# Chunk loop of a hybrid block: state-space output written channel by channel, two heads in the two column halves of TensorE, row factors loaded, no transposes of y

## The reference, cut to what matters

```python
lmat = jnp.exp(jnp.where(causal, seg, -jnp.inf))
scores = jnp.einsum('bclgn,bcsgn->bcgls', cc, bc)
y_diag = jnp.einsum('bcgrls,bcsgrp->bclgrp', scores[:, :, :, None] * lmat, xc)
...
y_off = jnp.einsum('bclgn,bcgrpn,bcgrl->bclgrp', cc, prev, jnp.exp(a_cum))
return (y_diag + y_off).reshape(bsz, s, h, pd)
...
y = y + d_skip.astype(f32)[:, None] * xh
y = y.reshape(bsz, s, SSM_D_INNER) * jax.nn.silu(z.astype(f32))
```

## Time and profile before

| | |
|---|---|
| median of 3 runs | 2541.73 us (2538.14 to 2541.93) |
| profiled execution, span from first to last instruction | 2534.6 us |
| its own time beyond the span | no row gives it; the runs' median stands 7.1 us above the span |
| TensorE busy | 2436.9 us, 96% of the span |
| VectorE, GpSimd, ScalarE busy | 1538.6, 1266.1, 822.5 us |
| mean granted TensorE clock | 0.989 of full |

### The profile page before, as it was taken

The page is one execution under the profiler, slowest core; times in us unless marked ns, Lnnn a source line. Parts: engine busy times, 40 slices in busy tenths (PEclk is TensorE's granted clock), DMA queues, the critical chain, the costliest instruction groups (busy, mean ns, idle before and its releaser), DMA issues. The chain is left out here.

```text
span 2534.6 us, 29658 instructions
## 1 busy us (share of the span) xinstructions
PE 2436.9 (96%) x11540; PEld 2011.4 (79%) x11540; DVE 1538.6 (61%) x1411; ACT 822.5 (32%) x965; POOL 1266.1 (50%) x687
## 2 busy tenths in 40 slices
PE   7999999899999999989999899999999999999998
PEld 6888887677778888878878678888888878888776
DVE  4977997325766567653244897677677652323575
ACT  5234443445412232331013543333333321000332
POOL 2337887544445455443353266556556543333563
PEclk9999999999999999999999999999999999999999
DMA  6222334698676667745232222222222243122332
GB/s 230 92 84 92 108 120 135 216 267 283 202 209 168 187 173 215 178 141 174 100 133 83 100 83 75 74 98 75 74 97 76 100 174 116 50 83 84 131 101 108
DMA packets 293607, 335.34 MB, mean 132 GB/s; under 512 B 44461, under 2 KB 249594, under 8 KB 289402
## 3 DMA queue, kind: packets, MB, share of 16 engines
q1 hardware_dynamic: 260650, 271.42, 34.4%
q10 hardware_dynamic: 32848, 62.40, 6.7%
HBM read 230.50 MB, written 103.28 MB: 132 GB/s over the span
## 5 line engine op out<-in xcount | busy, mean ns | idle before, releaser
L498 PE MATMUL ps<-act_hi,w_hi 128*128 128x512 f32 x1328 | 532.4, 401 | 13.3 <-ACT ring_b L1212 4.8
L483 POOL TENSOR_SCALAR w_hi<-w_raw 128x1024 fp32r<-128x1024 f32 x123 | 145.0, 1179 | 764.0 <-issue 688.4
L502 PE MATMUL ps<-act_hi,w_lo 128*128 128x512 f32 x1328 | 518.4, 390 | 0.0
L501 PE MATMUL ps<-act_lo,w_hi 128*128 128x512 f32 x1328 | 517.9, 390 | 0.0
L485 POOL TENSOR_TENSOR w_lo<-w_raw,w_hi 128x1024 fp32r<-128x1024 f32 x123 | 328.6, 2672 | 10.3
L498 PEld LDWEIGHTS ps<-act_hi,w_hi 128*128 128x128 f32 x1328 | 250.0, 188 | 71.6 <-issue 8.1
L502 PEld LDWEIGHTS ps<-act_hi,w_lo 128*128 128x128 f32 x1328 | 249.8, 188 | 53.1
L501 PEld LDWEIGHTS ps<-act_lo,w_hi 128*128 128x128 f32 x1328 | 250.1, 188 | 52.3 <-issue 3.3
L2036 POOL TENSOR_TENSOR w_lo<-sm,w_hi 128x512 fp32r<-128x512 f32 x120 | 209.1, 1743 | 113.9 <-ACT w_hi L2390 113.9
L2036 POOL TENSOR_TENSOR w_lo<-w_raw,w_hi 128x512 fp32r<-128x512 f32 x90 | 139.3, 1549 | 151.8 <-ACT w_hi L2390 151.8
L2152 PE MATMUL ps<-t,w_hi 128*128 128x512 f32 x480 | 186.9, 389 | 0.2 <-POOL w_lo L2036 0.2
(11 more groups left out here) (393 smaller groups left out, 5130.9 us busy)
## 6 DMA issues: line engine op xcount, KB each, us to landing
w_raw<-in_w_in_dram SPq DMA_DIRECT2D x34, 1024.0 KB, 6.0
spill<-ring_a ACTq DMA_DIRECT2D x36, 512.0 KB, 2.6
w_raw<-in_w_ffn_down_dram SPq DMA_DIRECT2D x18, 1024.0 KB, 5.0
w_raw<-in_w_ffn_up_dram SPq DMA_DIRECT2D x16, 1024.0 KB, 5.2
w_raw<-in_w_ffn_gate_dram SPq DMA_DIRECT2D x16, 1024.0 KB, 5.2
f_cm<-ring SPq DMA_DIRECT2D x32, 512.0 KB, 2.6
spill<-ring_b ACTq DMA_DIRECT2D x31, 512.0 KB, 6.9
qkv_a<-spill SPq DMA_DIRECT2D x7, 1536.0 KB, 8.4
```

The lines of the kernel that those rows point to most:

```text
L483: nc.gpsimd.tensor_scalar(hi, raw, 1.0, 0.0, ALU.mult, ALU.add).then_inc(split_done, 1)
L498: first = nc.tensor.matmul(o, wh, mov[0][:, k, c], start=(k == 0), stop=False)
L501: nc.tensor.matmul(o, wh, mov[1][:, k, c], start=False, stop=False)
L502: last = nc.tensor.matmul(o, wl, mov[0][:, k, c], start=False, stop=(k == KD - 1))
```

## The change

- `diag` now has `xc[:, h]` (64 columns) as stationary and `dec[:, h]` as moving operand; head h writes output partitions 0 to 63 or 64 to 127 by its parity. All 16 heads stand in one piece. `off` gives channels on partitions too, as 8 products instead of 2.
- The factor `exp(a_cum)` is no longer per partition. So ScalarE writes it once, ahead of the loop, to a scratch tensor `exp_rows`, and SP loads 8 rows of it to each half of `zt`, repeated over 64 partitions (`load_e`). `zt` is used twice a chunk: first for this factor, then for z, whose load moves up in the queue.
- VectorE adds `diag` in one instruction; the 8 transposes and their semaphore go.

```diff
@@ PE
-        def diag(c, g):
-            for i in range(HPG):
-                h = g * HPG + i
-                last = t.matmul(bank(PB, 2)[:, i * P:(i + 1) * P], dec[:, h, :],
-                                xc[:, h - h % 2:h - h % 2 + 2, :].rearrange("p h d -> p (h d)"), start=True, stop=True)
+        def diag(c):
+            for h in range(SSM_HEADS):
+                d = slice(SSM_HEAD_DIM * (h % 2), SSM_HEAD_DIM * (h % 2) + SSM_HEAD_DIM)
+                last = t.matmul(bank(PB, 2)[d, h // 2 * P:(h // 2 + 1) * P], xc[:, h, :], dec[:, h, :], start=True, stop=True)
             last.then_inc(diag_done, 1)
...
-            for g in range(SSM_GROUPS):
-                last = t.matmul(bank(PC + g), xbc[:, KD + 2 + g, :], of_group(s_ssm, g), start=True, stop=True)
+            for k in range(KD):
+                last = t.matmul(bank(PC, 2)[:, k * P:(k + 1) * P], s_ssm[:, 2 * k:2 * k + 2, :].rearrange("p h d -> p (h d)"),
+                                xbc[:, KD + 2 + k // 4, :], start=True, stop=True)
...
-            diag(c, 0)
+            diag(c)
             gemm(steps[1])
-            after(pe, y_sum, c * 3 + 2)
-            diag(c, 1)
+            after(pe, y_sum, c * 2 + 1)
...
-            after(pe, o_sum, c * 2 + 2)
-            for k in range(KD):
-                last = t.transpose(bank(PA, 2)[:, k * P:(k + 1) * P], ysum[:, k * P:(k + 1) * P], ident[:, :])
-            last.then_inc(yt_done, 1)
...
-                after(pe, y_mid, c * 2 + 1)
+                after(pe, o_sum, c * 2 + 2)
                 scores(c + 1)
@@ SP
         def load_dec(c):
-            after(sp, diag_done, c * 2)
+            after(sp, diag_done, c)
...
+        def load_e(c):
+            after(sp, y_mid, c * 2)
+            for i in range(2):
+                rows = exp_rows[ROW_DT + i:ROW_DT + SSM_HEADS:2, tokens(c)]
+                sp.dma_start(zt[64 * i:64 * i + 64, :, :], rows.unsqueeze(0).broadcast_to([64, KD, P])).then_inc(in_e, 16)
+
         def load_z(c):
-            after(sp, y_mid, c * 2)
+            after(sp, y_sum, c * 2 + 1)
...
                 load_bv(c + 1)
+            load_z(c)
             if c in blocks_at:
                 block_load(blocks_at[c])
             if c < NCH - 1:
                 load_dec(c + 1)
                 load_kd(c + 1)
                 load_mq(c + 1)
-                load_z(c + 1)
+                load_e(c + 1)
@@ DVE
-            after(dve, yt_done, c)
-            v.tensor_tensor(hd(ysum[:, :]), hd(bank(PC, 2)), wide(head_cols(c, EXP_D, SSM_HEADS), SSM_HEAD_DIM),
-                            ALU.mult).then_inc(y_sum, 1)
-            after(dve, y_sum, c * 3 + 1)
-            add_diag(c, 0)
-            add_diag(c, 1)
+            after(dve, in_e, c * 32 + 32)
+            after(dve, y_mid, c * 2)
+            v.tensor_tensor(hd(ysum[:, :], KD), hd(bank(PC, 2), KD), zt[:, :, :], ALU.mult).then_inc(y_sum, 1)
+            after(dve, diag_done, c + 1)
+            after(dve, y_sum, c * 2 + 1)
+            v.tensor_tensor(ysum[:, :], bank(PB, 2), ysum[:, :], ALU.add).then_inc(y_sum, 1)
...
-            after(dve, yt_done, c + 1)
+            after(dve, y_sum, c * 2 + 2)
             after(dve, xd_ready, c + 1)
-            v.tensor_tensor(yssm[:, :, :], hd(bank(PA, 2), 8), yssm[:, :, :], ALU.add).then_inc(y_mid, 1)
+            v.tensor_tensor(yssm[:, :, :], hd(ysum[:, :], KD), yssm[:, :, :], ALU.add).then_inc(y_mid, 1)
@@ ACT and DVE ahead of the loop
             act.dma_start(cum_rows, hrow[:, 1, :]).then_inc(cum_kept, 16)
+            a(hrow[:, 0, :], hrow[:, 1, :], ACT.Exp).then_inc(tm_act, 1)
+            act.wait_ge(tm_act, 5)
+            act.dma_start(exp_rows, hrow[:, 0, :]).then_inc(cum_kept, 16)
...
-        dve.wait_ge(cum_kept, 16)
+        dve.wait_ge(cum_kept, 32)
```

More of the change, by code:

```diff
@@ L52, in hybrid_block_kernel @@
     cum_rows = scratch("cum_rows", [P, SEQ])
+    exp_rows = scratch("exp_rows", [P, SEQ])
     y_cm = scratch("y_cm", [16, P, SEQ])
@@ L322, in hybrid_block_kernel @@
     blocks_in, sub_step, d_kept, tm_kept = sem("blocks_in"), sem("sub_step"), sem("d_kept"), sem("tm_kept")
-    in_xbc, in_qk, in_bv, in_kd, in_mq, in_dec, in_z, in_g, in_nt, in_d = (
-        sem(n) for n in ("in_xbc", "in_qk", "in_bv", "in_kd", "in_mq", "in_dec", "in_z", "in_g", "in_nt", "in_d"))
+    in_xbc, in_qk, in_bv, in_kd, in_mq, in_dec, in_e, in_z, in_g, in_nt, in_d = (
+        sem(n) for n in ("in_xbc", "in_qk", "in_bv", "in_kd", "in_mq", "in_dec", "in_e", "in_z", "in_g", "in_nt", "in_d"))
     ys_kept, yg_kept = sem("ys_kept"), sem("yg_kept")
@@ L330, in hybrid_block_kernel @@
         sem(n) for n in ("zeroed", "seg_done", "xd_ready", "xcd_ready", "s_ssm_dec", "s_gdn_dec"))
-    r_done, h_done, xt_done, sc_done, ks_done, qs_done, off_done, vn_done, ds_done, o_done, diag_done, st_done, yt_done, \
+    r_done, h_done, xt_done, sc_done, ks_done, qs_done, off_done, vn_done, ds_done, o_done, diag_done, st_done, \
         yssq_done, ot_done = (
             sem(n) for n in ("r_done", "h_done", "xt_done", "sc_done", "ks_done", "qs_done", "off_done", "vn_done", "ds_done",
-                             "o_done", "diag_done", "st_done", "yt_done", "yssq_done", "ot_done"))
+                             "o_done", "diag_done", "st_done", "yssq_done", "ot_done"))
     r_copied, bs_copied, dec_exp, vn_copied, osq_done, ysq_done, orst_done, yrs_done = (
@@ L846, in hybrid_block_kernel @@
     GIVEN = {
-        "sp": (a_in, a_dn[0], a_dn[1], a_dq[0], a_dq[1], in_xbc, in_qk, in_bv, in_kd, in_mq, in_dec, in_z, in_g, in_nt, in_d),
+        "sp": (a_in, a_dn[0], a_dn[1], a_dq[0], a_dq[1], in_xbc, in_qk, in_bv, in_kd, in_mq, in_dec, in_e, in_z, in_g, in_nt, in_d),
         "pool": (a_seg, seg_done, xd_ready, xcd_ready, s_ssm_dec, s_gdn_dec),
         "pe": (a_sum, a_gram, a_vt, a_kt, r_done, h_done, xt_done, sc_done, ks_done, qs_done, off_done, vn_done, ds_done, o_done,
-               diag_done, st_done, yt_done, yssq_done, ot_done),
+               diag_done, st_done, yssq_done, ot_done),
         "act": (a_sq, a_rs, a_exp, kept_qk, kept_bk, kept_d[0], kept_d[1], kept_n[0], kept_n[1],
@@ L958, in sp_mixer @@
         load_mq(0)
-        load_z(0)
+        load_e(0)
         block_load(2)
@@ L1145, in main @@
             last.then_inc(st_done, 1)
-            after(pe, y_sum, c * 3 + 3)
+            after(pe, y_sum, c * 2 + 2)
             if more:
                 invert_r(c + 1)
-            after(pe, o_sum, c * 2 + 2)
-            for k in range(KD):
-                last = t.transpose(bank(PA, 2)[:, k * P:(k + 1) * P], ysum[:, k * P:(k + 1) * P], ident[:, :])
-            last.then_inc(yt_done, 1)
             gemm(steps[3])
@@ L1301, in scale_x @@
             after(dve, xt_done, c + 1)
-            after(dve, diag_done, c * 2)
+            after(dve, diag_done, c)
             after(dve, xcd_ready, c)
@@ L1320, in mix_scores @@
                 v.tensor_tensor(dec[:, g * HPG:(g + 1) * HPG, :], dec[:, g * HPG:(g + 1) * HPG, :], s, ALU.mult).then_inc(m_ready, 1)
[L1322 to L1326, removed]
         def main(c, more):
@@ L1645, in sp_a @@
         sp.wait_ge(tm_kept, len(TM_COLS))
-        sp.wait_ge(cum_kept, 16)
+        sp.wait_ge(cum_kept, 32)
         past(sp, c_prod, PRODUCTS * C_PAIRS)
@@ L1799, in hybrid_block_kernel @@
     prod_done, w_high, w_low, w_sums = (later(sc_done, NCH), later(osq_done, NCH), later(seg_done, 2 * NCH), later(x_scaled, NCH))
-    copied, evicted = later(bs_copied, NCH), later(y_sum, 3 * NCH)
+    copied, evicted = later(bs_copied, NCH), later(y_sum, 2 * NCH)
     t_raw, t_high, t_low = later(o_normed, NCH), later(ysq_done, NCH), later(o_ssq, NCH)
```

## The result

The changed kernel takes 2546.06 us, the kernel before 2539.49 us (medians of 20 runs each). The ratio is 1.003, 95% interval 1.0019 to 1.004: **slower, by some 7 us**. The forecast was 2544, no change that can be told. The profiled executions are closer to each other than the medians: spans of 2534.6 and 2538.0 us. That of the changed kernel, 2539.71 us, is the fastest of its 20, so the profile shows about half of the difference.

A forecast was written before the change was run, and what follows sets the result against it. Two nearly equal bounds were assumed: TensorE's work and a loop of GpSimd's mask work, the DMA queue and dec's load. Saved TensorE work and mask delays summed to +2.2 us on 2541.7, giving 2543.9, say 2544; range 2526 to 2555.

The forecast's parts named there:

- Halves side by side, transposes gone, 2.6 us a chunk: TensorE, each chunk: mask products in two column halves take 1.79 us instead of 3.58, and 0.79 of transposes goes.
- The closed loop through `dec` bounds the late chunks: Chunk loop: GpSimd frees xbc, queued ahead of dec, which starts GpSimd; 43 us, nearly equal to TensorE's work.
- z ahead of `dec`, 1.5 us a chunk: DMA queue: z now precedes dec, which lands 1.5 us later in 7 chunks; earlier issue regains up to 1.5 without weight block.
- Factor rows of 6 us that hold up no engine: DMA queue after mq: repeated factor rows take 6 us, but their first reader comes over 18 us after z's use.
- "0 to 1 us, I take 0.3" for the second store: Ahead of the loop: VectorE waits for a second store until about 160 instead of 157.55; cost 0.3 us after slack.
- TensorE's added waits would be for `rhs`: Late chunks: TensorE's idle time rises about 3 us a chunk, released by VectorE's rhs.
- The sum, +2.2: Whole kernel: chunk walk with 3 us of fuller queue, less 1.8 in chunk 7, plus 0.3 ahead of the loop.
- the sum's own range: Whole kernel: -3 to +5 us, from queue delays (-3, +3), mask products at old pace (+1.8), dec's early issue (-1.5).
- the fuller queue decides: Rival, chance 0.28: repeated rows, stores and small loads outlast the loop queue's rest, delaying each chunk; 7 to 20 us slower.
- The range: Whole kernel's time: from 2526 us, with a tenth of the chance below, to 2555 above.
- the likeliest case: Whole kernel: the closed loop holds with small delays, time within 0.2%, 2539 to 2549 us; chance 0.38.

The follow-up runs named there:

- e6: Kernel before, with dec loaded as 1 MB without repeated rows from another tensor and its exponential scaled by 0.001 (values not the reference's): ratio 0.9924.
- e9: Kernel before, with dec's 16 rows also stored chunk by chunk, so its load repeats one 8 KB piece to all partitions: ratio 0.992.
- e8: e5 with the factor rows loaded into ysum, z's load back behind mq: ratio to the kernel before 1.0004.
- e5: Changed kernel; factor rows' exponential first, only their 16 used rows stored, sums' store issued first, first factor load behind two weight blocks: 1.0019 of the kernel before.
- e12: e11 with GpSimd's mask work held back until VectorE's last product with z of the chunk before: 0.9884 of the kernel before, 2510.18 us.
- e11: e8 with both repeated loads, dec and factor rows, read from one-piece-per-chunk sources (8 KB; 4 KB per half): 0.9925 of the kernel before.

## Why the prediction was right and wrong

**Halves side by side, transposes gone, 2.6 us a chunk:** right (1.89 us for 32 records; 3.64 in one half).

**The closed loop through `dec` bounds the late chunks:** right in kind, and larger than I had it. I called TensorE and the loop "nearly equal", with 3.5 us of room in two early chunks; e6 and e9 took 19 and 20 us off the kernel before by `dec` alone. I took TensorE's 2 idle us in each of two windows for little. Over the 350 us of the loop they are 17.8. Where e6 gains, GpSimd shows: from chunk 0's mask to chunk 1's are 75.7 us before (724.50 to 800.21) and 68.5 in e6 (722.06 to 790.56), 7 us, and from there to the last `skip_x` 290.6 and 282.4, 8 us.

**z ahead of `dec`, 1.5 us a chunk:** right where a weight block stands in the queue. From the issue of `xbc` to GpSimd's start on `dec` these five chunks take 1.5 us more on average (the last 24.6 for 22.4, forecast 24). The two chunks without a block take 2.3 and 0.7 us less, where I had at best even: the earlier issue of `dec` is worth more than the 1.5 us that I allowed it. GpSimd's wait grows by 1.0 a chunk over the seven. e8 undid that and stands 4.6 us lower, but it moves the factor rows as well.

**Factor rows of 6 us that hold up no engine:** right in the chunks as to their own reader, wrong for the first one, which I never placed in the queue ahead of the loop. TensorE's wait there went from 1.60 and 2.74 to 7.11 us.

**"0 to 1 us, I take 0.3" for the second store:** the step that failed most plainly. The landing was as I estimated (160.83, "about 160"), but I counted only VectorE's own slack. The shift laid more of its instructions beside GpSimd's, one took 4.37 us for 3.02, and TensorE waited 2.8. In the profiled executions this and the first factor load delayed the first mask product by 7.9 us; with e5 nothing of it is left.

**TensorE's added waits would be for `rhs`:** wrong, those are 3.4 us for 4.4 before. They are for `ring_b`, whose eviction stands behind the mask's exponential on ScalarE. I had followed the mask only forward, to its readers, and not asked what waits behind the engine that waits for it.

**The sum, +2.2:** measured are +6.6 by the medians. That the forecast of 2544 lies so near to 2546 is in part luck. It stands on a median of 3 runs, 2541.73, and 20 runs gave 2539.49. Its 7.1 us beyond the span are no time of the kernel's own: in every run with both numbers the time is 1.7 to 1.9 us above its own span, and the rest is the difference between executions. The +5 of the sum's own range is the sum of its bounds, but the -3 should be -4.5.

The sum's terms left out TensorE's clock. By the products of time and clock the changed kernel is 2 us faster; by the mean clocks, 0.9878 and 0.9834, some 11 us (0.0044 of 2540) go the other way. The stops of 5.4 and 7.11 us are each followed by work at half pace, so the windows show the clock fall behind stops. In the two profiled executions (0.989 and 0.985) it is also clear where: 1.00 to 0.98 in 770 to 1120 us, some 7 us, and 0.98 to 0.93 in 700 to 770 us, 3.5 us. For the runs as a whole it stays open. e5 took the two stops ahead of the loop away or down and kept a mean of 0.9833, and e12, without a stop from 790 to 1075 us, has the same 0.9868 as e11 with its stops.

Of the rivals, "the fuller queue decides" had the sign, and a size (2547 to 2560) just above the 2546 measured, but not the place: in the loop GpSimd waited only 1.0 us a chunk longer for `dec`, and the slow rows did their harm at the first load, ahead of the loop. The range held the time; the likeliest case did not hold the sign.

## What to carry to other kernels

Work taken off the busiest engine is only had if nothing else bounds it, and if not it becomes a stop, which may cost the clock on top. Read the clock beside the busy time, and time times clock over several runs. Before costing a late result, list what stands behind each in-order engine that waits for it, and what its instructions will then run beside. Price a repeated load by how its source lies: 8 KB in one piece took 7.4 us, 16 rows apart 17.5.

## What the runs showed of the hardware that was not expected

- The 1 MB load of `dec`: 17.5 us from issue to landing as 16 separate rows of 512 bytes repeated, 7.4 as one repeated piece of 8 KB, 7.0 without repeating. The Trainium skill (DMA: Bandwidth & Descriptors, Specifications) has 512 bytes as enough for full line rate; for repeated rows the measurement decides otherwise. Rows of 512 bytes that are not repeated do move fast here (`xbc`, 768 KB in 5.7 us).
- Eight copies, each read by 16 partitions, moved at 186 GB/s against 403 for the single one, with the DMA engines' share at 1.03 and 0.98; the cause was not tested.
- VectorE's 128x1024 product of two SBUF operands: 1.22 us alone, up to 5.49 beside GpSimd; with one operand in PSUM 1.21 to 1.23 in every group read in e9, e11 and e12. In e11 both slow instructions of a chunk end 1.1 us after GpSimd's.
- After TensorE stood for 5.4 us: granted clock 0.50, a filler product every 0.43 us for 0.23.
